# Two thirds of the second block's modulation moved out of the experts' routing and into the attention of its first mixer

## What is computed

```
# first block, layer 0 and 1
mod = silu(c) @ mod_w[layer] + mod_b[layer]
sh1, sc1, g1, sh2, sc2, g2 = split(mod, 6)
x = x + g1 * mixer(rms_norm(x) * (1 + sc1) + sh1)
x = x + g2 * moe(rms_norm(x) * (1 + sc2) + sh2)      # 16 experts, top 2
# second block, layer 0 and 1, also over 256 rows of context (xc)
mod, mod_c = silu(c2) @ w_mod[l] + b_mod[l], silu(c_ctx) @ w_mod[l] + b_mod[l]
y, yc = mixers(x * (1 + sc1) + sh1, xc * (1 + sc1c) + sh1c)
x = layer_norm(a * x + g1 * y); x = layer_norm(a * x + g2 * mlp(x * (1 + sc2) + sh2))
```

## Time and profile before

| | us |
|---|---|
| median of three runs | 1893.97 |
| fastest and slowest of them | 1890.2, 1894.23 |
| the profiled execution, time | 1888.88 |
| its span | 1887.1 |
| TensorE busy | 1718.4 (91%) |
| VectorE busy | 974.3 (52%) |
| ScalarE busy | 632.9 (34%) |
| moved by DMA | 430.06 MB, mean 228 GB/s |

### The profile page before, as it was taken

One profiled execution on the slowest core, in us unless ns is written; L12 is line 12 of the kernel. 1 busy time (PEld: TensorE's weight loads), 2 busy tenths in 40 slices (PEclk: granted clock), 3 DMA queues, 4 the chain that ended last, 5 costly groups with the idle time before them and its releaser, 6 DMA issues.

```text
span 1887.1 us, 22744 instructions
## 1 busy us (share of the span) xinstructions
PE 1718.4 (91%) x9160; PEld 1187.9 (63%) x9160; DVE 974.3 (52%) x1837; ACT 632.9 (34%) x1099; POOL 13.3 (1%) x14
## 2 busy tenths in 40 slices
PE   6999877999998779989988999999999799889998
PEld 5665632444675324447545778888888674678886
DVE  5883400103344000145577586887667857675555
ACT  2142111112322111123356545222233425655443
POOL 0000000000000000000000000000000100000000
PEclk9999888999999889999999989999999899999999
DMA  9978799999957999992100113455454120034540
GB/s 388 404 289 332 292 404 421 421 420 421 372 219 322 410 406 418 420 385 89 67 23 1 39 52 134 156 196 205 179 197 183 52 105 23 23 124 160 186 157 23
DMA packets 62901, 430.06 MB, mean 228 GB/s; under 512 B 6592, under 2 KB 10816, under 8 KB 10944
## 3 DMA queue, kind: packets, MB, share of 16 engines
q1 hardware_dynamic: 62784, 428.48, 56.9%
HBM read 427.40 MB, written 1.05 MB: 227 GB/s over the span
## 4 chain that ended last, share of the span: by engine, by line
PE 66%; DVE 14%; DMA 10%; ACT 7%; issue 2%; SPq 1%; DVEq 0%; ACTq 0%
PE bank L292 14%; PE bank L1144 13%; PE bank L296 8%; PE bank L298 8%; PE bank L297 8%; DMA ring<-in_ws_dram 8%; DVE ring_halves L2549 3%; PE bank L331 3%; ACT work_halves L2543 2%; DMA work<-in_ws_dram 2%; DVE work L438 1%; PE bank L2162 1%; PE bank L2185 1%; PE bank L2657 1%; ACT work L2296 1%
## 5 line engine op out<-in xcount | busy, mean ns | idle before, releaser
L296 PE MATMUL bank<-work_halves 128*128 128x512 f32 (+1 forms) x1088 | 394.6, 363 | 17.0 <-DVE HH_halves L2012 4.8
L298 PE MATMUL bank<-work_halves,ring_halves 128*128 128x512 f32 (+1 forms) x1088 | 387.1, 356 | 0.0
L297 PE MATMUL bank<-HH_halves,work_halves 128*128 128x512 f32 (+1 forms) x832 | 287.7, 346 | 0.0
L1144 PE MATMUL bank<-ring,work 128*32 128x512 f32 (+2 forms) x896 | 258.5, 659 | 19.8 <-DMA work<-in_ws_dram 9.1
L1144 PE MATMUL bank<-work 128*32 128x512 f32 (+2 forms) x640 | 221.5, 644 | 36.1 <-DMA ring<-in_ws_dram 35.0
L296 PEld LDWEIGHTS bank<-work_halves 128*128 128x128 f32 x1088 | 208.5, 192 | 52.2 <-DVE HH_halves L2012 6.6
L298 PEld LDWEIGHTS bank<-work_halves,ring_halves 128*128 128x128 f32 x1088 | 208.2, 191 | 28.4
L2549 DVE TENSOR_TENSOR ring_halves<-ring,work_halves 128x2048 fp32r<-128x2048 f32 x72 | 163.5, 2288 | 48.0 <-ACT work_halves L2543 47.9
L297 PEld LDWEIGHTS bank<-HH_halves,work_halves 128*128 128x128 f32 x832 | 160.5, 193 | 19.9 <-issue 1.7
L1422 DVE TENSOR_TENSOR work<-work,bank 128x512 f32<-128x512 f32 x14 | 9.6, 687 | 302.9 <-PE bank L1144 302.9
L1144 PEld LDWEIGHTS bank<-work 128*32 128x32 f32 (+2 forms) x640 | 61.7, 137 | 133.5 <-issue 131.0
(11 more groups left out here) (382 smaller groups left out, 2560.7 us busy)
## 6 DMA issues: line engine op xcount, KB each, us to landing
ring<-in_ws_dram SPq DMA_DIRECT2D x287, 1024.0 KB, 11.0
work<-in_ws_dram SPq DMA_DIRECT2D x117, 1024.0 KB, 18.5
con<-in_con_dram SPq DMA_DIRECT2D x1, 1177.0 KB, 27.4
XX<-in_xT_dram SPq DMA_DIRECT2D x1, 1024.0 KB, 9.7
XX<-in_cT_dram SPq DMA_DIRECT2D x1, 1024.0 KB, 19.0
out_dram<-XX SPq DMA_DIRECT2D x1, 512.0 KB, 3.6
out_dram<-XX SPq DMA_DIRECT2D x2, 256.0 KB, 2.7
par<-in_par_dram SPq DMA_DIRECT2D x1, 338.0 KB, 3.1
```

What stands on the lines that cost most here:

```text
L296: pe.matmul(out, l[0], r[0], start=start, stop=False)
L297: pe.matmul(out, l[0], r[1], start=False, stop=False)
L298: return pe.matmul(out, l[1], r[0], start=False, stop=stop)
L1144: m = pe.matmul(b[c, :], left[:, k, c], ring_of(self.w[i])[:, 512 * k:512 * k + 512], start=first and k == 0, stop=last and k == 3, skip_g ...
```

## The change

The thirds are dealt out anew. `first` has four thirds, all done before `moe0`; `second` has `mods[1]` third 2 and `mods[2]` third 0 in the same 20 steps of the norm and the odd mixer; `third`, with a row buffer in `work`, has `mods[2]` thirds 1 and 2, and its 20 steps stand in the attention of `mix0`, two per iteration from i = 8 to 17. The two routings have none. Bank 7 joins the rotation of the scores at i = 18, not 8. `dve_affine` of `ffn0` moves to i = 18.

```
-                self.steps = range(first, first + 4), range(first + 4, 10 * len(bg.thirds))
+                end = 10 * len(bg.thirds)
+                self.steps = range(first, min(first + 4, end)), range(first + 4, end)
...
-                        put(0, (0, 1, 2) if both else (0, 1, 2, 7), "s", u)
+                        put(0, (0, 1, 2) if both or self.steps(i) else (0, 1, 2, 7), "s", u)
...
+                for i in range(len(self.between)):
+                    for s in self.steps(i):
+                        self.mods.plan(s)
+
+            def steps(self, i):
+                return (2 * i - 16, 2 * i - 15) if self.mods and 8 <= i < 18 else ()
...
+                    if self.mods and i == 19:
+                        self.M.wait_mod(pe, 2)
...
+                    for s in self.steps(i):
+                        self.mods.pe(pe, s)
...
+                    for s in self.steps(i):
+                        self.mods.act(act, s)
...
                         st.wait_ge(act, "qrope", 6)
+                        if self.mods:
+                            self.M.st.wait_ge(act, "turned", 2)
                         self.ffn.split_act(act, 0)
...
+                    if self.mods and i == 8:
+                        for ev in sum(self.between, []):
+                            if self.ro.of[ev][0] == 7:
+                                st.wait_ge(dve, "evicted", ev)
+                        self.mods.begin(dve)
+                    if self.mods and i == 18:
+                        self.ffn.dve_affine(dve)
...
+                    for s in self.steps(i):
+                        self.mods.dve(dve, s)
...
-        first = Behind(spare, (mods[0], 1), (mods[0], 2), (mods[1], 0), (mods[1], 1), (mods[1], 2))
+        first = Behind(spare, (mods[0], 1), (mods[0], 2), (mods[1], 0), (mods[1], 1))
...
-        second = Behind(spare, (mods[2], 0), (mods[2], 1), (mods[2], 2))
+        second = Behind(spare, (mods[1], 2), (mods[2], 0))
+        third = Behind(k8(work[:, WORK - 1016:WORK - 504], 256), (mods[2], 1), (mods[2], 2))
...
-        mix0 = Mix(0, mods[2], Dotted(mods[3], "dot", 1, 13312, 4))
+        mix0 = Mix(0, mods[2], Dotted(mods[3], "dot", 1, 13312, 4), third)
```

More of the change, by code:

```diff
@@ L1580, in dve @@
                 self.by_place(dve, self.gate, self.gates, "gates")
-                self.bg.thirds[-1][0].wait_mod(dve, 2)
+                M, g = self.bg.thirds[-1]
+                M.wait_mod(dve, g)
                 for i in range(4):
@@ L1832, in build, with __init__ @@
         class Mix:
-            def __init__(self, l, M, bg):
-                self.l, self.last, self.M, self.bg = l, l == 1, M, bg
+            def __init__(self, l, M, bg, mods):
+                self.l, self.last, self.M, self.bg, self.mods = l, l == 1, M, bg, mods
                 self.st = st = stage(f"mix{l}")
@@ L2737, in act @@
                 act.activation(small[:, 248:249], ones[:, 0:1], ACT.Sqrt)
+                self.M.wait_mod(act, 1)
                 for k in range(8):
@@ L3161, in build @@
         ffn0.plan()
-        mix1 = Mix(1, mods[3], None)
+        mix1 = Mix(1, mods[3], None, None)
         ffn0.next = mix1
@@ L3196, in sync_program @@
                     moe1.st.wait_ge(sp, *moe1.used(0, 0))
-                    mods[2].wait_mod(sp, 2)
+                    mods[2].wait_mod(sp, 0)
                     sp.dma_start(XX[:, :, 256:512], d["cT"]).then_inc(s_ctx, 16)
@@ L3256, in vector_program @@
             mix0.split_dve(dve, 2)
-            ffn0.dve_affine(dve)
             mix0.dve(dve)
```

## The result

| | before | after |
|---|---|---|
| median, us | 1893.31 (4 runs) | 1903.66 (4 runs) |
| fastest and slowest | 1890.2, 1894.23 | 1902.55, 1905.87 |
| profiled execution, time / span | 1888.88 / 1887.1 | 1904.44 / 1902.7 |

The ratio is 1.0054 with a 95% interval of 1.0037 to 1.0070; the forecast was 1905.0 (1.0058). The two profiled executions lie 15.6 us apart, the medians 10.3.

The account below looks back on a forecast made before the run. DMA was taken to bound the expert stages and TensorE the attention. Experts -1.4 us and attention +12.5 gave +11.1 us on a median of 1893.97, so 1905 us, with a range of 1896.5 to 1911.

Parts of the forecast that it names:

- The start of the stream: Ahead of the experts: DMA already idles at 1 GB/s before the counts, so removing sixteen chunks starts no stream earlier; gain 0.
- rival (a): Expert stages: each chunk removed brings the weight stream forward 2.49 us, 39.9 less 12.5, giving 1867 us; chance 0.07.
- The clock in the routing: Both routings: TensorE idles before the mask, its clock falls, and the last small products slow; 0.7 us each, +1.4 for two.
- The norm and odd mixer: Between the expert stages: as many steps as before in the same places; zero, apart from the shift by `moe0`'s gain.
- TensorE's earlier start: After the counts: TensorE gets to the experts 4.1 us earlier in the first stage, some 2.4 in `moe1`.
- The holes: DMA stream early in both expert stages: TensorE's earlier start closes holes of 2.0 and 0.8 us, -2.8 in all.
- beyond that the stream is full and gives nothing: Expert stages: once the first hole is closed, a still earlier TensorE brings no further gain.
- The ten iterations: Attention, i = 8 to 18: 15.7 us of steps on 31.5 of TensorE work, 47.2 against 34.8, so +12.4 us.
- The drain: Attention: tiling mode changes drain TensorE; taken as inside the 1.82 us per two chunks; if felt, the attention's term grows.
- `dve_affine`: Attention, i = 18: its six operations and the flush are nearly covered by the turn in i = 17; +0.1 us.
- Together: The whole attention: the ten iterations' +12.4 us and +0.1 for `dve_affine`, taken as +12.5 us.
- Rival (b): Attention takes 15.7 us in full, with new bank waits or drains; clock falls in both routings; +17 to +20, 1912; chance 0.18.

Follow-up runs that it names:

- cover: The changed kernel with three groups of four filler matmuls in both routings, between the transposes and the wait for the mask; ratio to before 1.0055.
- covertail: The kernel of cover with seven more filler groups in the routings, behind the product that the counts come from; ratio to before 1.0078.
- again: The changed kernel unaltered, run and traced once more; median 1903.73 us, ratio to before 1.0051.
- noatt: The changed kernel without the attention's sixteen chunks, neither loaded nor multiplied; clearing, copy of rows, turn and flush stay; ratio to before 1.0011.
- quarter: The changed kernel with one of the four matmuls of each chunk in the attention, all loads and waits kept; ratio to before 1.0058.
- attwarm2: The changed kernel with filler matmuls ahead of the transposes, two groups in i = 21 and three in i = 23; ratio to before 1.0065.
- warm: The kernel of cover with fillers also in three waits of the first round of experts (6, 3 and 2 groups of four); ratio to before 1.0045.

## Why the prediction was right, step by step

- **The start of the stream: right.** DMA stands at 0 GB/s ahead of the first load by count in the first routing of every trace; `mix0` started 2.1 us sooner in after, not 10 (1.4 of it is the start), and rival (a) is out.
- **The clock in the routing: right in kind, half the size.** Forecast 0.7, measured 1.38 to 1.49 in the first routing in all eight traces that empty it without cover, and none of it with cover. There the fall came at the first sums, not late in them. In the second routing it is -0.1 to +1.5, 0.6 in the mean of eight traces, and -0.2 with cover: the clock fell late in the sums in after (at 592.8 us, 0.3 ahead of the small product), as the forecast had it. So this cost is not certain in every routing, as the prediction took it to be.
- **The norm and odd mixer: zero was not zero.** The same steps in the same places took -0.1 to +1.7 us more, by where the clock fell. The forecast had no term for this.
- **TensorE's earlier start: a step was missed.** 4.1 and 2.4 us were forecast; counted from the small product it starts 3.1 and 2.0 us earlier (9.97 against 13.07, 9.52 against 11.49). It no longer waits for its own instructions but for VectorE clearing the banks (L1585), a new releaser that the earlier trace rows already showed for `moe1`.
- **The holes: wrong term.** Both closed in their place, but 2.0 us in the first stage were worth 0.3 in the stream and nothing at its end; in the second the 0.8 went with a gain of about 3, of which covertail ties 1.6 to the earlier start and the other half has no known cause. The step that failed is "beyond that the stream is full and gives nothing": it was not full (308 and 328 GB/s at 250 and 260 us). The slots of the eight chunks in flight are freed by TensorE, and after its longer wait (6.94 us in after, 2.95 before) it used the second group in 5.2 us instead of 4.7, 4.4 of them at 1.2 GHz (3.4 before). The two errors and the clock's nearly cancel, which is luck and not a sum that held: from the logits to the scores of i = 8 the sum was to be -1.4; it is -0.4 in after, +0.4 in again, -0.8 and -1.0 in noatt and quarter.
- **The ten iterations: right mechanism, 2.2 us too much.** TensorE is the bound and waits once, 0.3 us. Added: 8 x 1.83 + 0.39 for the turn inside and 0.39 for that of i = 17, 15.4 us. Its own work is then 45.0 - 15.4 = 29.6 us, not the 31.5 read from the earlier trace rows. Those later periods have no wait in brackets, but the same work takes 9.54 us a period there and 9.0 with the steps taken off here (13.03 - 2 x 1.83 - 0.39; 14.50 - 3 x 1.83): eight transposes take 1.22 us against 1.04, and what follows starts later by 0.16 to 0.18 in three places. Small waits sit inside the rows. The slack was 5.2 us, not 3.3. The drain that the Trainium skill (TensorEngine Tiling (Array Packing), "Key Properties") speaks of left no mark beyond this: 1.83 us between 128-column products here, 1.82 in the odd mixer.
- **`dve_affine`: 0.1 was 0.7 to 0.9.** It stands in VectorE's queue ahead of the maxima of i = 18, and those are late next.
- **Together** the attention is +10.9 us (again, quarter, cover, attwarm2) against 12.5 forecast; 15.1 in after and warm, where the clock falls behind the second split. Rival (b) had nearly the right size for after's own trace, but not by its reasons (no wait for a bank, no drain). With -0.5 ahead of it, the mean of seven traces of the whole edit without cover, the sum is +10.4; the medians say +10.3 and +10.0. This agreement is not a check. The sum leaves out the rest, +2.3 to +3.9 in nine traces of the whole edit and -0.1 in quarter, and it is taken against a trace of before that lies 4.4 us under that kernel's median; what the median execution has more was not traced. The mechanism in the attention is shown; that the total came within 1 us is partly luck.

## What to carry to other kernels

Work that fills an idle time of TensorE is free where it stands, and it keeps the clock for the small products behind it. Before moving it to a stage where the same engine is the bound, price it there at its full time less the engine's real slack. Take the slack from rows with work packed in, since rows without a reported wait can still hold small ones. When the slots of a stream are freed by the engine that waits for it, closing a hole is no gain until the next holes have been read too: follow the slots to the stage's end. And compare a sum of stretches with the medians only after asking how far each profiled execution lies from its own median.

## What the hardware showed

- TensorE's clock was found low behind waits of about 3 us (3.15 in the first routing), and not behind all of them (3.13 at 1557.3 us in before: not; 3.13 at 1569.7 in after: low). Which work then runs at 1.2 GHz moves between executions of one kernel (after and again), by 4 us in one place of the attention.
- Four matmuls of two columns into four row groups of a bank took as long as one: 1.90 and 1.88 us for two chunks.
- Filler of 7.9 us ahead of the reading of the count delayed what followed by more than itself: a wait called issue in the gathering grew from 0.82 to 2.99 us. Its cause was not looked into.
